# Differential attention in a two-block transformer kernel: the normalisation works on the accumulator, and an output unit gets a bank of its own

## The reference, cut to what matters

```
def diff_attention(q1, q2, k1, k2, v, lam):      # per head, chunk-causal mask
    p1 = softmax(where(mask, q1 @ k1.T * scale, -inf))
    p2 = softmax(where(mask, q2 @ k2.T * scale, -inf))
    return (p1 - lam * p2) @ v

o = diff_attention(...)                           # 256 x 6 x 128
o = rmsnorm(o, subln, eps=1e-5) * (1 - lam_init)  # over the 128 of each head
x = x + concat(o, memory_attention) @ w_o         # 1024 x 1024
x = x + square(relu(rmsnorm(x) @ w_up)) @ w_down  # the last MLP follows
```

## Time and profile before

| | |
|---|---|
| median of 3 runs | 1104.34 us (1100.55, 1104.34, 1104.52) |
| profiled execution, its own time | 1100.11 us |
| span in the profile | 1098.3 us |
| mean granted TensorE clock | 0.988 |
| PE busy | 1049.3 us, 96% of the span |
| DVE, ACT, POOL busy | 649.4, 542.2, 374.8 us |

### The profile page before, as it was taken

How to read it: one execution, slowest core, us unless ns; L and a number is a source line. 1 busy time by engine, 2 the same in 40 slices (tenths; PEclk the granted TensorE clock), 3 DMA queues, 4 the chain that set the end, 5 groups by cost and what they waited for, 6 DMA issues and landing times.

```text
span 1098.3 us, 19678 instructions
## 1 busy us (share of the span) xinstructions
PE 1049.3 (96%) x8492; PEld 1019.1 (93%) x8492; DVE 649.4 (59%) x836; ACT 542.2 (49%) x756; POOL 374.8 (34%) x196
## 2 busy tenths in 40 slices
PE   3999999998999999989999999999999989999998
PEld 1799999998999999989999999999898879999998
DVE  6968668656666455617765444445766656544443
ACT  2478677543665444634344444444655535444341
POOL 4038377332565342541202342231522312342221
PEclk9999999998999999989999999999999899999999
DMA  9987577544667554524546555556532225665541
GB/s 330 316 269 249 182 242 267 170 138 154 210 213 238 184 192 154 192 77 154 169 155 213 166 185 188 184 192 185 154 115 78 77 81 174 207 192 185 167 148 39
DMA packets 169860, 197.37 MB, mean 180 GB/s; under 512 B 5380, under 2 KB 137901, under 8 KB 169645
## 3 DMA queue, kind: packets, MB, share of 16 engines
q1 hardware_dynamic: 169772, 196.11, 55.1%
HBM read 195.03 MB, written 1.06 MB: 179 GB/s over the span
## 4 chain that ended last, share of the span: by engine, by line
PE 86%; DVE 6%; ACT 4%; issue 2%; DMA 1%; POOL 1%; DVEq 1%; SPq 0%; ACTq 0%; POOLq 0%
PE bank L512 85%; DVE w_lo L1801 2%; ACT w_hi L1234 1%; DMA xT<-in_x 1%; POOL stat L1763 1%; PE bank L782 0%; DMA ada_raw<-in_w_ada 0%; ACT h_hi L1328 0%; DVE y_tok L2352 0%; DVE big L2221 0%; ACT h_hi L1269 0%; ACT ada_raw L1224 0%; ACT big L1281 0%; DVE big L2209 0%; DVEq L2247 0%
## 5 line engine op out<-in xcount | busy, mean ns | idle before, releaser
L1801 DVE TENSOR_TENSOR w_lo<-w_raw,w_hi 128x2048 fp32r<-128x2048 f32 x158 | 389.0, 2465 | 247.5 <-ACT w_hi L1234 246.2
L512 PE MATMUL bank<-h_hi,w_hi 128*128 128x256 f32 x1328 | 374.2, 288 | 9.2 <-DVE w_lo L1801 5.0
L512 PE MATMUL bank<-h_hi,w_lo 128*128 128x256 f32 x1328 | 369.0, 285 | 0.0
L1234 ACT ACTIVATE w_hi<-w_raw 128x2048 fp32r<-128x2048 f32 x158 | 301.1, 1908 | 128.2 <-PE bank L512 121.1
L512 PE MATMUL bank<-h_lo,w_hi 128*128 128x256 f32 x1328 | 346.4, 284 | 0.0
L512 PE MATMUL bank<-u_hi,w_hi 128*128 128x256 f32 x1024 | 289.5, 286 | 4.2 <-ACT u_hi L1243 2.7
L512 PE MATMUL bank<-u_hi,w_lo 128*128 128x256 f32 x1024 | 287.1, 284 | 0.0
L512 PE MATMUL bank<-u_lo,w_hi 128*128 128x256 f32 x1024 | 277.0, 284 | 0.0
L1614 POOL TENSOR_TENSOR u_lo<-fresh,u_hi 128x512 fp32r<-128x512 f32 x60 | 142.2, 2372 | 393.5 <-ACT u_hi L1243 393.4
L512 PEld LDWEIGHTS bank<-h_hi,w_hi 128*128 128x128 f32 x1328 | 256.1, 193 | 15.3 <-issue 8.3
L512 PEld LDWEIGHTS bank<-h_hi,w_lo 128*128 128x128 f32 x1328 | 256.1, 193 | 0.0
(11 more groups left out here) (254 smaller groups left out, 996.9 us busy)
## 6 DMA issues: line engine op xcount, KB each, us to landing
w_raw<-in_w_mlp SPq DMA_DIRECT2D x32, 1024.0 KB, 5.4
w_raw<-in_w_up SPq DMA_DIRECT2D x32, 1024.0 KB, 5.4
w_raw<-in_w_down SPq DMA_DIRECT2D x32, 1024.0 KB, 5.0
w_raw<-in_w_in SPq DMA_DIRECT2D x21, 1024.0 KB, 6.4
ada_raw<-in_w_ada SPq DMA_DIRECT2D x19, 1024.0 KB, 7.6
w_raw<-in_a_w_in SPq DMA_DIRECT2D x10, 1024.0 KB, 5.1
w_raw<-in_w_o SPq DMA_DIRECT2D x8, 1024.0 KB, 5.1
w_raw<-in_w_out SPq DMA_DIRECT2D x4, 1024.0 KB, 5.2
```

Source lines behind the costliest of these rows:

```text
L512: return pe.matmul(dst, lhsT, rhs, start=start, stop=stop, skip_group_check=True)
L1234: act.activation(w_hi[:, n % PARTS_RING, :], w_raw[:, slot_of[n], :], ACT.Copy).then_inc(hi_w, 1)
L1801: dve.tensor_tensor(w_lo[:, n % PARTS_RING, :], w_raw[:, slot_of[n], :], w_hi[:, n % PARTS_RING, :].bitcast(F32), ALU.subtract).then_inc(l ...
```

## The change

`o_copy` goes. `o_square` reads the result of `pv` in `ps_misc`, and `o_scale` reads it there too, multiplies it by the root and writes `y_tok`; `misc_read` is raised by `o_scale`. `turn_o` writes to `acc[3]`, with semaphores of its own (`o_turned`, `o_taken`), and the `oT` entries leave `MISC`. Unit 124 (`N_O1 + 2`) gets a third bank, `lin[2]`, which is `acc[2]` under another name; it stands outside the alternation of the two others and is run in quarters as well. The step lists of PE, ACT, POOL and DVE are reordered: `o_part` now takes one unit per call, and the quarters of units 122 to 124 are placed between the last heads. Left out below is the renaming of the semaphores.

```diff
--- before.py
+++ after.py
@@ -158,8 +158,8 @@
 MISC = (["sum1", "row", "wi"] + [f"fox{g}" for g in range(4)]
         + [f"dsa{g}" for g in range(4)] + ["sum2", "summem", "memspread", "sum3", "qk.mem0", "qk.qm0", "mem0.0", "mem0.1",
            "qk.mem1", "sum5", "sum6",
-           "qk.k0", "qk.qm1", "qk.q0", "mem1.0", "qk.k1", "mem1.1", "qk.q1", "pv0", "pv1", "oT0", "qk.k2", "oT1", "qk.q2",
-           "pv2", "pv3", "oT2", "oT3", "pv4", "pv5", "oT4", "oT5", "sum7"])
+           "qk.k0", "qk.qm1", "qk.q0", "mem1.0", "qk.k1", "mem1.1", "qk.q1", "pv0", "qk.k2", "pv1", "qk.q2", "pv2", "pv3",
+           "pv4", "pv5", "sum7"])
 ROPES = ("k0", "q0", "k1", "q1", "k2", "q2")
 
 ROOTS = [m for m in MISC if m[:3] in ("sum", "qk.")]
@@ -241,10 +241,12 @@
     lin_bank, before, evac_value = [], [], []
     emptied, order = {"a": 0, "v": 0}, []
     for n, (_, _, _, user) in enumerate(units):
-        lin_bank.append(len(order) % 2 if user else None)
-        before.append(order[-2] if user and len(order) >= 2 else None)
+        alone = n == N_O1 + 2
+        lin_bank.append(2 if alone else len(order) % 2 if user else None)
+        before.append(order[-2] if user and not alone and len(order) >= 2 else None)
         if user:
             emptied[user] += 1
+        if user and not alone:
             order.append((user, emptied[user]))
         evac_value.append(emptied[user] if user else None)
 
@@ -345,7 +347,7 @@
         bank = [ctx.enter_context(nc.psum_tensor(f"bank{i}", [P, 512], F32)) for i in range(8)]
-        lin, acc, ps_ada, ps_misc = bank[0:2], bank[2:6], bank[6], bank[7]
+        lin, acc, ps_ada, ps_misc = bank[0:2] + bank[4:5], bank[2:6], bank[6], bank[7]
         mem_bank = [(acc[0], acc[1]), (ps_ada, acc[2])]
         bias_dram = nc.dram_tensor("bias_rows", (HEADS, 384), F32, kind="Internal").ap()
...
@@ -1059,12 +1061,15 @@
                 last.then_inc(misc_full, 1)
 
             def turn_o(h):
-                into_misc(f"oT{h}")
-                pe.wait_ge(o_scaled, h + 1)
+                pe.wait_ge(misc_read, misc_no[f"pv{h}"] + 1)
+                if h:
+                    pe.wait_ge(o_taken, h)
+                if h < 2:
+                    pe.wait_ge(spread_read, spread_no["qk.k2" if h else "qk.k1"] + 1)
                 c0 = 256 + (h % 2) * P
                 for tt in range(TT):
-                    last = pe.transpose(ps_misc[:, tt * P:tt * P + P], y_tok[:, tt, c0:c0 + P], ident)
-                last.then_inc(misc_full, 1)
+                    last = pe.transpose(acc[3][:, tt * P:tt * P + P], y_tok[:, tt, c0:c0 + P], ident)
+                last.then_inc(o_turned, 1)
 
             def m_scores(g):
                 for odd in range(2):
@@ -1117,12 +1122,14 @@
                 if tt:
                     last.then_inc(unit_done, 1)
 
-            def o_part(pair, job, first=False):
-                for m in range(2):
-                    if first:
-                        start_unit(N_O1 + m)
-                    pe.wait_ge(fresh_lo, job + 1)
-                    part(N_O1 + m, pair, u_hi, u_lo, first=first)
+            def o_part(m, pair, job, last=False):
+                n = N_O1 + m
+                if job == J_YM1:
+                    start_unit(n)
+                    if m == 2:
+                        pe.wait_ge(rope_read, len(ROPES))
+                pe.wait_ge(fresh_lo, job + 1)
+                part(n, pair, u_hi, u_lo, first=job == J_YM1, last=last)
 
             qk_squares("k0", N_K[0])
             rotate("k0", tiles_of("k0"))
@@ -1149,11 +1156,11 @@
             pe.wait_ge(misc_read, misc_no["mem1.1"] + 1)
             pe.wait_ge(spread_read, spread_no["qk.k0"] + 1)
             to_T(acc[3:4], y_tok, y_turned)
+
+            d_turn(0)
+            d_scores(1)
             rotate("q1", tiles_of("q1"))
             qk_squares("q1", N_Q[1])
-
-            d_turn(0)
-            d_scores(1)
             half_n(N_K[2], 0, h_hi, h_lo)
             pv(0)
             pe.wait_ge(fresh_ready, J_YM1 + 1)
@@ -1163,48 +1170,50 @@
             d_turn(1)
             d_scores(2)
             half_n(N_Q[2], 0, u_hi, u_lo)
+            qk_squares("k2", N_K[2])
+            rotate("k2", tiles_of("k2"))
+            turn_o(0)
+            half_n(N_Q[2], 1, u_hi, u_lo)
             pv(1)
-            rotate("k2", tiles_of("k2"))
-            half_n(N_Q[2], 1, u_hi, u_lo)
-            turn_o(0)
-            qk_squares("k2", N_K[2])
 
             d_turn(2)
             d_scores(3)
             half_tok(N_V[1], 0, h_hi, h_lo)
+            qk_squares("q2", N_Q[2])
             rotate("q2", tiles_of("q2"))
+            pe.wait_ge(o_taken, 1)
+            spread_qk("k2", acc[3])
             half_tok(N_V[1], 1, h_hi, h_lo)
-            turn_o(1)
-            qk_squares("q2", N_Q[2])
-            spread_qk("k2", acc[3])
             pv(2)
 
             d_turn(3)
             d_scores(4)
+            turn_o(1)
             half_tok(N_V[2], 0, h_hi, h_lo)
             pv(3)
+            turn_o(2)
             half_tok(N_V[2], 1, h_hi, h_lo)
-            turn_o(2)
 
             d_turn(4)
             d_scores(5)
-            o_part(3, J_YM1, first=True)
             turn_o(3)
+            o_part(0, 3, J_YM1)
+            o_part(1, 3, J_YM1)
             pv(4)
-            o_part(0, J_DIFF[0])
+            o_part(0, 0, J_DIFF[0])
+            o_part(1, 0, J_DIFF[0])
 
             d_turn(5)
+            o_part(0, 1, J_DIFF[1])
             pv(5)
+            o_part(1, 1, J_DIFF[1])
             turn_o(4)
-            o_part(1, J_DIFF[1])
+            o_part(2, 3, J_YM1)
             turn_o(5)
-            pe.wait_ge(fresh_hi, J_DIFF[2] + 1)
-            for m in range(2):
-                part(N_O1 + m, 2, u_hi, u_lo, products="h")
-            pe.wait_ge(fresh_lo, J_DIFF[2] + 1)
-            for m in range(2):
-                part(N_O1 + m, 2, u_hi, u_lo, last=True, products="l")
-            product(N_O1 + 2, u_hi, u_lo)
+            o_part(2, 0, J_DIFF[0])
+            o_part(2, 1, J_DIFF[1])
+            for m in range(3):
+                o_part(m, 2, J_DIFF[2], last=True)
             product(N_O1 + 3, u_hi, u_lo)
             mlp(N_MLP2, X_H7, J_MLP2, early=3, between={4: lambda: sum_x("sum7"),
                                                         5: lambda: spread_sum(7, ps_ada)})
@@ -1528,11 +1537,11 @@
                 act.activation(probsT[:, h % 2, 0:384], ps_ada[:, 0:384], ACT.Copy).then_inc(d_copied, 1)
 
             def o_square(h):
-                act.wait_ge(o_copied, h + 1)
+                act.wait_ge(misc_full, misc_no[f"pv{h}"] + 1)
                 for tt in range(TT):
-                    at, c0 = S_OSS + 2 * (h % 2) + tt, 256 + (h % 2) * P
-                    last = act.activation(o_squares[:, (h % 2) * T + tt * P:(h % 2) * T + tt * P + P], y_tok[:, tt, c0:c0 + P],
-                                          ACT.Square, accum_out=stat[:, at:at + 1])
+                    at = S_OSS + 2 * (h % 2) + tt
+                    last = act.activation(o_squares[:, (h % 2) * T + tt * P:(h % 2) * T + tt * P + P],
+                                          ps_misc[:, tt * P:tt * P + P], ACT.Square, accum_out=stat[:, at:at + 1])
                 last.then_inc(o_sq, 1)
 
             def mem_exps(g):
@@ -1564,36 +1573,36 @@
             split_w(N_K[2] + AHEAD)
             d_copy(0)
             d_exps(1)
+            o_square(0)
             evac_k(2)
 
             d_copy(1)
-            o_square(0)
             split_w(N_Q[2] + AHEAD)
             d_exps(2)
             evac_q(2)
+            o_square(1)
 
             d_copy(2)
-            o_square(1)
+            split_w(N_V[1] + AHEAD)
             split_h(J_YM1, u_hi, 6)
-            split_w(N_V[1] + AHEAD)
             d_exps(3)
             evac_v_unit(1)
+            o_square(2)
 
             d_copy(3)
-            o_square(2)
             split_w(N_V[2] + AHEAD)
-            split_h(J_DIFF[0], u_hi, 0)
             d_exps(4)
             o_square(3)
+            split_h(J_DIFF[0], u_hi, 0)
             evac_v_unit(2)
 
             d_copy(4)
             split_w(N_V[2] + AHEAD + 1)
             d_exps(5)
             o_square(4)
+            split_h(J_DIFF[1], u_hi, 2)
 
             d_copy(5)
-            split_h(J_DIFF[1], u_hi, 2)
             o_square(5)
             split_h(J_DIFF[2], u_hi, 4)
             split_w(N_O1 + AHEAD + 1)
@@ -1768,18 +1777,18 @@
             head_unit("q0")
             head_unit("k1")
             head_unit("q1")
+            o_power(0)
             cos_part("k2", flat(qk, 4, 6))
-            o_power(0)
             power("qk.k2")
             cos_part("q2", flat(big, 14, 16))
-            split_h(J_YM1, u_lo, u_hi, 6)
             o_power(1)
             power("qk.q2")
+            split_h(J_YM1, u_lo, u_hi, 6)
             o_power(2)
             split_h(J_DIFF[0], u_lo, u_hi, 0)
             o_power(3)
+            split_h(J_DIFF[1], u_lo, u_hi, 2)
             o_power(4)
```

(57 more changed lines are left out.)

## The result

The changed kernel takes 1092.66 us in the median of four runs (1091.21 to 1093.45); the kernel before, on the same chip, takes 1103.59. The ratio is 0.9907, with an interval of 0.9887 to 0.9926: faster by 0.9%, against a forecast of 1093 us. The profiled execution took 1091.21 us (forecast 1090.8), with a span of 1089.4 us where it was 1098.3, at a mean granted clock of 0.992 where it was 0.988.

What follows compares the result with a forecast made beforehand. PE, busy 96% of the span, was taken as the bound. Removed 9.7 + 4.5 = 14.2 us, new waits 4.9, net 9.3: 1100.11 becomes 1090.8, plus 2.1 gives 1093 us; range 1087 to 1102.

Steps and rivals of the forecast that it cites:

- All six waits: PE's idle time in the stage, by cause: 3.3, 3.2, 0.8, 0.7, 1.3 and 0.4 us, 9.7 us in all, removed.
- For the clock 4.5 us were taken: Two low-clock stretches in the stage, 4.5 us at 0.62 and 7.6 us at 0.55, would go: 4.5 us gained.
- the 1.5 us for restarts: Allowance in the range's lower bound for restarts after the removed gaps, left out of the sum: 1.5 us.
- pv(2): First new wait: it stands directly behind the half unit whose values it reads, with the evacuation uncovered: 0.95 us.
- qk_squares("q2"): Second new wait: ps_misc is held until o_scale has read it, 2.84 us against 2.88 of cover: 0.1 us taken.
- d_turn(5): Third new wait: DVE needs about 9.1 us for the work in front, PE some 8.2: 0.8 us, between 0 and 2.3.
- unit 125: Fourth new wait: its parts need unit 122's ring place, 4.45 us with only 2.88 of cover: 1.6 us.
- unit 127: Fifth new wait: second unit of the MLP, its bank free only after the last add_out: 1.45 us.
- At this size the source makes no difference: Claim that the new o_scale, reading the bank, costs what the old did from y_tok, 282 ns.
- The held power: Rival: DVE holds up POOL's power by 1.97 us at three places, net gain 3.4, time 1099; chance 0.10.
- The held bank: Rival: ps_misc held 4.25 us at all six heads by a split and a held power, time 1116; chance 0.06.
- The clock did not fall again: Rival denied here: remaining gaps bring low stretches costing 4.5 us again, gain 4.8, time 1097.5; chance 0.18.

Runs made afterwards that it cites:

- one gap of 1.70 us alone: The changed kernel with one added PE wait for the first head's take, before the second half of unit 119: 1095.01 us, ratio 0.9928.
- the filled gaps: The kernel before with thirteen matmuls that nobody reads, into acc[3], in seven places where PE had waited: 1103.47 us, ratio 1.0001.
- two gaps closed: The changed kernel with pv(2) behind the scores and unit 127's split ahead of the one it doesn't need: 1091.08 us, ratio 0.9910.
- three gaps closed: As two gaps closed, plus POOL's subtraction moved and unit 124's quarter that needs no split put first: 1092.14 us; beside the changed kernel 1090.09.

## Why the prediction was right, and where it was off

**What is removed.** All six waits are gone, 9.7 us, as the prediction put it. For the clock 4.5 us were taken, less than the 5.1 that half of each low stretch would be, because part of a short matmul is not array time. The spacing of the matmuls bears that out: 0.214 us in a low stretch against 0.120 at full clock, 44% lost and not half (last section), and 44% of 10.2 us is 4.5. The span leaves 8.9 - 3.9 = 5.0 us; what the other 0.5 us are no row shows. So there is no room for the 1.5 us for restarts in the lower bound of the range, which no run shows. In the mean of the executions the clock counts for more than half: on the chip of the last group the mean clock is 0.9844 over eleven executions of the kernel before and 0.9898 over four of the changed one, 0.0054 x 1100 = 5.9 us, and with 3.9 us of idle time that makes 9.8; the mean times differ by 9.9. But this clock is that of the whole span, and how much of it belongs to the stage is seen in the profiled executions alone.

**The five new waits.** All are where they were expected; forecast and measured: `pv(2)` 0.95 and 1.02, `qk_squares("q2")` 0.1 and none that PE's list shows, `d_turn(5)` 0.8 and 1.72, unit 125 1.6 and 1.78, unit 127 1.45 and 1.30. Together 4.9 and 5.8. The 0.9 us too little here and the 0.5 us too little for the clock have opposite signs, so the net gain, 9.3 us forecast and 8.9 by the span, came out closer than its largest error. The third is the term that was mis-sized, inside its own bounds (0 to 2.3): the working took a mix at its undisturbed 1.73 us, while POOL's subtraction, moved ahead of `o_power(4)` by the change, now falls on it. The prediction had priced this contention for the power and the mean, but not for the mix; moving POOL away took 1.04 us off that wait.

**Work from the bank.** "At this size the source makes no difference" was wrong. The scale, the mean and the power of the changed kernel, with the columns of the earlier trace rows:

```profile
L2354 DVE TENSOR_SCALAR y_tok<-bank,stat x12: 341/344/351, 838.4 to 882.8; 128x128 f32<-128x128 f32 x12
```

```profile
L1772 POOL TENSOR_TENSOR stat<-stat,minus_half x6: 695/695/697, 833.5 to 881.4; 128x2 f32<-128x2 f32 x6
```

A scale from the bank takes 344 ns in the median where it took 282: 62 ns more. Per pair that is about 0.13 us, and PE lists no wait for it at any head, so it cost nothing here. The rule of the Trainium skill that the prediction weighed (VectorE: DVE Perf Modes, Why PSUM operands drop a tier) has the right direction; its size as estimated there, up to 0.56 us for a pair, was not reached. That a copy from the bank took 282 ns was no measure for a scale from it.

**The rivals.** The held power fell: no power took longer than 697 ns, where the longest before took 2671. The held bank fell with it: PE lists no wait of a `pv` or `qk_squares` for line 2354; only two weight loads, ahead of `qk_squares("q2")` and `pv(3)`, stood for it, 0.5 us together. The clock did not fall again in the two profiles of the changed kernel, but the prediction's argument, that gaps behind 885 us bring none, does not hold in general: of eleven profiles of kernels with the new order the stage lost nothing in three, 1.7 us in six and 3.4 in two, always between 880 and 902 us.

**The middle of the runs.** The forecast added 2.1 us to the profiled execution's time; the median lies 1.45 above it. That this fits is luck: the 2.1 us are half the distance between two groups of runs of the kernel before, and nothing in them tells where the changed kernel's runs lie.

**Slips that carry nothing.** The two low stretches before begin 2.9 and 1.2 us behind the end of the wait ahead of them, not both 2 to 4. The twelve copies keep DVE busy for 3.0 us, not 3.4, since they overlap. The held bank would eat up the gain from (9.3 + 2.8) / 6 = 2.0 us at each head on, not 2.5. The terms of the lower bound give 1090.8 - 0.8 - 1.5 = 1088.5, not 1087.

**What stays open.** Why the low clock comes in one execution and not in the next. Filling the gaps raised the mean clock, one gap of 1.70 us alone brought no low stretch behind it, and in executions without a profile its place isn't seen. What the fourteen profiles show is where it came: each of the fourteen low stretches of the stage begins between 0.3 us before and 2.9 us behind the end of a PE wait of 1.43 to 2.63 us, and twelve other waits of 1.4 us or more were followed by none. The kernel before has three such waits, the changed one two (1.72 and 1.78 us), and with the filled gaps there is none. So that the changed kernel shows full clock in both of its profiles is in part luck: in the other nine with the new order, ten of seventeen such waits were followed by a low stretch.

## What to carry to other kernels

Where one engine is busy 96% of the span, list its idle times in the stage by what ends them, then follow each wait through the new order with the durations of the trace: here that gave four of five new waits within 0.2 us. Work taken from an engine that is not the bound was worth nothing that could be measured (0.3 us for twelve copies), and a bank of its own without a new order a third of the whole. When a step of POOL is moved, look at which DVE instructions with operands in the on-chip buffer it now falls on.

## What the runs showed of the hardware

What a low stretch costs: in the kernel before, the first low stretch of the stage in windows of 2 us:

```profile
848.00:850.00 2.00, 2.00 (x12) 1.44 (x11) 0.46 (x3) 1.67 (x7) 1.63 (x2) 0.93 0.01 4
850.00:852.00 2.00, 2.00 (x10) 2.00 (x11) 1.97 (x11) 2.00 (x2) 2.00 (x4) 0.50 0.00 0
852.00:854.00 2.00, 2.00 (x15) 2.00 (x14) 2.00 (x2) 1.84 (x8) 1.90 (x2) 0.72 0.00 0
```

By the clock 0.14 + 1.00 + 0.56 = 1.7 us are lost here. In this stage, in all the profiles, a low stretch came to 1.7 or 3.4 us by this sum. The matmuls lose a little less. In the kernel with two gaps closed a low stretch of 3.4 us falls into unit 125. Thirteen matmuls pass between the first two of these lines, twenty between the last two:

```profile
893.64 0.42 PE L514 MATMUL bank<-u_hi,w_hi 128*128 128x256 f32 x1
896.42 0.41 PE L514 MATMUL bank<-u_lo,w_hi 128*128 128x256 f32 x1
896.79 0.28 PE L514 MATMUL bank<-u_hi,w_hi 128*128 128x256 f32 x1
899.18 0.28 PE L514 MATMUL bank<-u_hi,w_lo 128*128 128x256 f32 x1
```

That is 2.78 / 13 = 0.214 us for one at the clock of 0.50 and 2.39 / 20 = 0.120 at 1.00.

Executions of one kernel lie up to 7.7 us apart, and for the kernel with the filled gaps the time goes with the mean clock: 1098.4 us at 0.992 and 1106.1 at 0.986. It doesn't everywhere: the changed kernel took 1094.8 us at 0.991 and 1093.1 at 0.987 on one chip, and its two profiles, with the same four waits and full clock in the stage, are 3.6 us apart in the span, which arises ahead of the stage. Differences of 2 us between kernels are only seen on one chip, with several runs of each.

A scale that reads the bank is not held by POOL's subtraction. In the changed kernel none of the twelve ran during one, but with POOL's subtraction moved a pair did (the subtraction, shown above, lasts from 879.22 to 880.48 us):

```profile
879.36 0.61 DVE L2354 TENSOR_SCALAR y_tok<-bank,stat 128x128 f32<-128x128 f32 x2 [0.88 <-POOL stat L1772]
```

It took 0.61 us, as the pair did without POOL beside it (878.73 us in the changed kernel). A pair that read `y_tok`, in the kernel before, took 1.50 us under the same kind of subtraction in place of 0.48:

```profile
868.73 1.50 DVE L2352 TENSOR_SCALAR y_tok<-y_tok,stat 128x128 f32<-128x128 f32 x2 [0.59 <-POOL stat L1763]
```

```profile
868.67 1.29 POOL L1614 TENSOR_TENSOR u_lo<-fresh,u_hi 128x512 fp32r<-128x512 f32 x1
```

Both profiles with three gaps closed show the same: 0.35 and 0.34 us for the two scales of a pair under a subtraction. So a scale from the bank was slower by 62 ns, and out of POOL's way.
